# Seven products instead of eight in four pairs of chunks of the second feed-forward input product, on one Trainium2 core

## What is computed

```python
    h = rmsnorm_2(x, g_ffn[l])
    u = causal_dwconv(h @ w_up[l], ffn_conv_w[l]) + ffn_conv_b[l]   # w_up: 2048 x 11264, conv over 3 positions
    gate, val = jnp.split(u, 2, axis=-1)
    x = x + (jax.nn.silu(gate) * val) @ w_down[l]
```

## Time and profile before

| | before |
|---|---|
| median of three runs | 2409.65 us (2408.84 to 2410.35) |
| the profiled execution | 2408.56 us |
| its span, first to last instruction | 2406.8 us |
| TensorE busy in the span | 2396.3 us (10618 matmuls) |
| DVE busy | 1724.7 us (72%) |
| ACT busy | 1343.0 us (56%) |
| TensorE clock | 0.999 |

### The profile page before, as it was taken

How to read it: one execution, slowest core, us unless ns; L and a number is a source line. 1 busy time by engine, 2 the same in 40 slices (tenths; PEclk the granted TensorE clock), 3 DMA queues, 4 the chain that set the end, 5 groups by cost and what they waited for, 6 DMA issues and landing times.

```text
span 2406.8 us, 27970 instructions
## 1 busy us (share of the span) xinstructions
PE 2396.3 (100%) x10618; PEld 1984.3 (82%) x10618; DVE 1724.7 (72%) x2122; ACT 1343.0 (56%) x1641; POOL 190.1 (8%) x349
## 2 busy tenths in 40 slices
PE   9999999999999999999999999999999999999998
PEld 8888888888888888888888888888888888888887
DVE  7575555666778888669786865786577766678886
ACT  7555566445555555445455754555566666665554
POOL 0000000001000000000001110111111111110000
PEclk9999999999999999999999999999999999999999
DMA  8777666678767777776668777887788888886664
GB/s 276 224 222 231 195 189 185 215 240 247 221 215 220 230 222 218 226 220 210 198 223 274 247 236 218 254 246 236 236 244 248 243 242 239 243 239 208 219 217 158
DMA packets 155446, 545.86 MB, mean 227 GB/s; under 512 B 20144, under 2 KB 20656, under 8 KB 155184
## 3 DMA queue, kind: packets, MB, share of 16 engines
q1 hardware_dynamic: 131552, 470.91, 62.2%
q0 software_dynamic: 23184, 72.37, 11.4%
q10 hardware_dynamic: 576, 0.79, 0.1%
HBM read 505.72 MB, written 38.27 MB: 226 GB/s over the span
## 4 chain that ended last, share of the span: by engine, by line
PE 93%; DVE 4%; DMA 1%; ACT 1%; issue 1%; SPq 0%; ACTq 0%; DVEq 0%
PE ps L1851 92%; DMA raw<-in_w_ffn_in 1%; DVE wl L1287 1%; DVE tmp L1315 0%; DVE wl L1324 0%; ACT wh L933 0%; ACT wh L957 0%; ACT tmp L973 0%; DVE gated_lo L1301 0%; DVE tmp L1318 0%; DVE tmp L1320 0%; DVE ps L1393 0%; PE ps L1989 0%; DMA XG<-in_x 0%; DVE tmp L1592 0%
## 5 line engine op out<-in xcount | busy, mean ns | idle before, releaser
L1287 DVE TENSOR_TENSOR wl<-raw,wh 128x1024 fp32r<-128x1024 f32 x794 | 966.0, 1222 | 620.4 <-ACT wh L933 619.0
L933 ACT CAST wh<-raw 128x1024 fp32r<-128x1024 f32 x794 | 829.2, 1049 | 769.4 <-PE ps L1851 760.5
L1851 PE MATMUL ps<-wh,x4g_hi 128*128 128x512 f32 x704 | 273.9, 389 | 0.0
L1851 PE MATMUL ps<-wl,x4g_hi 128*128 128x512 f32 x704 | 273.9, 389 | 0.0
L1851 PE MATMUL ps<-wh,x4g_lo 128*128 128x512 f32 x704 | 273.9, 389 | 0.0
L1851 PE MATMUL ps<-wh,x1g_hi 128*128 128x512 f32 x592 | 230.3, 389 | 0.0
L1851 PE MATMUL ps<-wl,x1g_hi 128*128 128x512 f32 x592 | 230.3, 389 | 0.0
L1851 PE MATMUL ps<-wh,x1g_lo 128*128 128x512 f32 x592 | 230.3, 389 | 0.0
L1851 PE MATMUL ps<-wh,h_hi 128*128 128x512 f32 x576 | 225.2, 393 | 0.6 <-ACT wh L938 0.6
L1851 PE MATMUL ps<-wh,h_lo 128*128 128x512 f32 x576 | 223.8, 391 | 0.0
L1851 PE MATMUL ps<-wl,h_hi 128*128 128x512 f32 x576 | 223.4, 390 | 0.0
(11 more groups left out here) (378 smaller groups left out, 3954.6 us busy)
## 6 DMA issues: line engine op xcount, KB each, us to landing
raw<-in_w_in SPq DMA_DIRECT2D x196, 512.0 KB, 4.3
raw<-in_w_ffn_in SPq DMA_DIRECT2D x176, 512.0 KB, 4.3
raw<-in_w_up SPq DMA_DIRECT2D x176, 512.0 KB, 4.7
raw<-in_w_ffn_out SPq DMA_DIRECT2D x88, 512.0 KB, 4.2
raw<-in_w_down SPq DMA_DIRECT2D x88, 512.0 KB, 4.2
rows<-Y POOLq DMA_DIRECT2D x67, 512.0 KB, 4.9
Z<-rows POOLq DMA_DIRECT2D x268, 128.0 KB, 5.0
raw<-in_w_o SPq DMA_DIRECT2D x32, 512.0 KB, 4.3
```

The costliest lines, as they stand in the source:

```text
L933: e.copy(wh[:, i % RING, :], raw[:, slot, :]).then_inc(rounded, 1)
L1287: e.tensor_tensor(wl[:, r, :], raw[:, i % RAW, :], wh[:, r, :].bitcast(F32), ALU.subtract).then_inc(remainder, 1)
L1851: return e.matmul(dst, weights, x, start=start, stop=stop, skip_group_check=True)
```

## The change

Pairs 1, 3, 5 and 7 of the up product (chunks 2, 3, 6, 7, 10, 11, 14, 15) are laid out side by side, with units at row pairs 4 and 6 of the eight. In pair 1 the two units are steps 3 and 5 (counted from 0) of six common steps; in the others they are steps 1 and 3 of four. The four banks 4 to 7 take the pair, 0 to 3 the shared products. The up stage gets tiles of its own for bases, sums and x forms. `shared_bank` is planned in the step s of `plan_up`, before `UP_LATE` is added; `UP_LATE` moves what follows chunk 3 three steps later, chunks 6, 10 and 14 one, chunks 7, 11 and 15 two, leaves chunk 1 at four, and takes the two steps of chunk 2 away. The host reorders the weights of the four pairs. The down product's first pair now waits for `up_rows` 14 and 15 for its banks.

```diff
-SEVEN = {"gated": (4, 6), "out1": (8, 10, 12, 14, 16, 18), "down": (8, 10, 12, 14, 16, 18)}
+SEVEN = {"gated": (4, 6), "up": (4, 6), "out1": (8, 10, 12, 14, 16, 18), "down": (8, 10, 12, 14, 16, 18)}
...
+UP_PAIRS = (1, 3, 5, 7)
+UP_ORDERS = {1: (0, 1, 2, 4, 3, 6, 5, 7), 3: (0, 4, 1, 6, 2, 3, 5, 7), 5: (0, 4, 1, 6, 2, 3, 5, 7), 7: (0, 4, 1, 6, 2, 3, 5, 7)}
+UP_TAILS = {1: 6, 3: 4, 5: 4, 7: 4}
+UP_LATE = {1: 4, 2: 0, 3: 3, 6: 1, 7: 2, 10: 1, 11: 2, 14: 1, 15: 2}
...
+        up_hi = view("up_hi", [P, 3, 512], o_b + 28 * K, FR)
+        up_lo = view("up_lo", [P, 3, 512], o_b + 74 * K, FR)
+        up_sums = view("up_sums", [P, 4, 512], o_b + 80 * K)
+        up_xs_hi = view("up_xs_hi", [P, 2, 4, P], o_b + 34 * K, FR)
+        up_xs_lo = [view(f"up_xs_lo{i}", [P, 4, P], o_b + at * K, FR) for i, at in enumerate((38, 72))]
...
@@ -533,7 +545,9 @@
         def plan_up(n):
             def after(s, chunk):
                 chunk.drained = [("up_rows", n)]
-                s += (0, 4, 2)[n] if n < 3 else 0
+                s += UP_LATE.get(n, 0)
+                if n // 2 in UP_PAIRS:
+                    do("shared_bank", "up", n)
...
-        for n in range(2, 22):
-            last_up = product(t["w_up2"], "N", "ffn2", PAIRS16, ("up", n), plan_up(n), n)
+        plan_x_sums("up", len(granules), 0)
+        for q in range(1, 11):
+            if q in UP_PAIRS:
+                cleared = [[("pool_out", 1)], [("x_split", 1, 1)]] if q == 1 else [[("up_rows", 2 * q - 4 + n)] for n in range(2)]
+                product_side_by_side(t["w_up2"], "up", q, 4, UP_ORDERS[q], UP_TAILS[q], [plan_up(2 * q), plan_up(2 * q + 1)], 0, cleared,
+                                     ("shared_out", "shared_sums", "shared_last"))
+                continue
+            for n in (2 * q, 2 * q + 1):
+                last_up = product(t["w_up2"], "N", "ffn2", PAIRS16, ("up", n), plan_up(n), n)
+                if q - 1 in UP_PAIRS:
+                    last_up.cleared = [("shared_out", "up", q - 1)]
...
-            cleared = ([("pool_out", 1)], [("x_split", 1, 1)]) if q == 0 else ([("shared_out", "down", 0)],) * 2
+            cleared = ([("up_rows", 14)], [("up_rows", 15)]) if q == 0 else ([("shared_out", "down", 0)],) * 2
...
+        def up_at(n):
+
+            return at("shared_bank", "up", n) if n // 2 in UP_PAIRS else product_of("up", n)
...
-                    e.wait_ge(*product_of("up", n))
+                    e.wait_ge(*up_at(n))
...
+                    elif unit.pair.stage == "up":
+                        if unit.pair.q > UP_PAIRS[0]:
+                            e.wait_ge(*at("shared_bank", "up", 2 * unit.pair.q - 3))
...
+                    if stage == "up":
+                        e.tensor_tensor(up_xs_lo[0][:], up_out[:, 0], up_xs_hi[:, 0].bitcast(F32), ALU.subtract)
+                        e.tensor_tensor(up_xs_lo[1][:], up_out[:, 1], up_xs_hi[:, 1].bitcast(F32),
+                                        ALU.subtract).then_inc(done[name], 1)
+                        continue
...
-                    n, = args
-                    bank0, bank1 = banks(named["gated", n])
-                    e.wait_ge(*product_of("gated", n))
+                    stage, n = args
+                    tile_sums = tile_sums_of[stage]
+                    bank0, bank1 = banks(named[stage, n])
+                    e.wait_ge(*product_of(stage, n))
```

More of the change, by code:

```diff
@@ L810, in two_slots @@
             return x[:, i % RING:i % RING + 2, :].rearrange("p r c -> p (r c)")
-        bases = {"gated": (gated_hi, gated_lo), "out1": (base_hi, base_lo), "down": (base_hi, base_lo)}
-        x_places = {"gated": (gated_in, gated_out), "out1": (xs_in, xs_out), "down": (xs_in, xs_out)}
+        bases = {"gated": (gated_hi, gated_lo), "out1": (base_hi, base_lo), "up": (up_hi, up_lo),
+                 "down": (base_hi, base_lo)}
+        x_places = {"gated": (gated_in, gated_out), "out1": (xs_in, xs_out), "up": (up_in, up_out),
+                    "down": (xs_in, xs_out)}
         def all_three(x):
@@ L821, in x_forms @@
                 return [[x[:, unit.place, n] for x in (gated_xs_hi, gated_xs_lo)] for n in range(4)]
+            if unit.pair.stage == "up":
+                return [[x[:, n] for x in (up_xs_hi[:, unit.place], up_xs_lo[unit.place])] for n in range(4)]
             k = 2 * unit.p
@@ L956, in scalar @@
                     e.wait_ge(*at("sums", i))
+                    tile_sums = tile_sums_of[seven[i].pair.stage]
                     e.copy(two_slots(wh, i), tile_sums.rearrange("p k c -> p (k c)")).then_inc(done[name], 1)
@@ L972, in scalar @@
                     for k, place in enumerate((0, 3, 2, 1)):
-                        e.copy(tile_sums[:, place, :], ps[:, pair.shared + k, :]).then_inc(done[name], 1)
+                        e.copy(tile_sums_of[stage][:, place, :], ps[:, pair.shared + k, :]).then_inc(done[name], 1)
                 elif name == "first_hi":
@@ L1357, in vector @@
                     stage, q = args
-                    p1, p7, p6, _ = (tile_sums[:, k, :] for k in range(4))
+                    p1, p7, p6, _ = (tile_sums_of[stage][:, k, :] for k in range(4))
                     e.wait_ge(*at("shared_out", stage, q))
@@ L1364, in vector @@
                     stage, q = args
-                    _, second, first, p5 = (tile_sums[:, k, :] for k in range(4))
+                    _, second, first, p5 = (tile_sums_of[stage][:, k, :] for k in range(4))
                     e.wait_ge(*at("shared_sums", stage, q))
@@ L1390, in vector @@
                     else:
-                        b = named["gated", n].bank
-                        e.wait_ge(*at("shared_last", "gated", n // 2))
+                        b = named[stage, n].bank
+                        e.wait_ge(*at("shared_last", stage, n // 2))
                         e.tensor_tensor(ps[:, b:b + 2, :], ps[:, b:b + 2, :], tile_sums[:, 2:4, :], ALU.add).then_inc(done[name], 1)
```

35 lines of the change are left out of this document (21 added, 14 removed).

## The result

| | before | changed |
|---|---|---|
| median | 2409.52 us (4 runs) | 2439.19 us (4 runs, 2436.54 to 2440.95) |
| profiled execution | 2408.56 us | 2440.95 us |
| span | 2406.8 us | 2439.1 us |
| matmuls | 10618 | 10594 |
| TensorE clock | 0.999 | 0.994 |

The changed kernel is 1.0121 times as long (95% interval 1.0109 to 1.0133): **29.7 us slower**, where 2436, 26.5 more, was forecast.

The account below looks back on a forecast made before the run. TensorE was taken to bound the kernel, 93% of the chain that ended last. 31.9 us of waits less 5.4 saved gave +26.5 on 2409.65, thus 2436 us; range 2411 to 2450.

Parts of the forecast that it names:

- sum of waits: TensorE waits in all four pairs: 3.0 in pair 1, 12.7 in pair 3, 16.2 in pairs 5 and 7.
- Saving: Eight steps of the pairs, 21 matmuls each in place of 24: 5.4 us saved on TensorE's path.
- up_rows 9 at 12.2: Pair 5: up_rows 9 ends 12.2 us after TensorE starts the pair, wanted at 5.4: a wait of 6.8 us.
- the walk's first event: Pair 5: up_first 6 on ACT starts 23.0 us before TensorE begins the pair.
- this costs nothing: Weight fetches: SP's wait for base_lo, with later fetches behind it, delays no weight TensorE needs; cost 0.
- Second units of pairs 5 and 7: Second seven-product step of each pair: TensorE, already 6.8 late, waits 1.2 us more for base_lo or forms_lo.
- Pair 3: Waits of 0.1 us at the second granule, 6.9 at the first unit, 5.7 at the second: 12.7 us.
- Pair 1: No wait at its units; three late splits behind it of 0.6, 1.25 and 1.1 us: 3.0 us.
- B: Rival: the walked waits hold and the clock falls in the long waits: 2446 us; chance 0.20.
- A: Rival: the walked waits hold at the high clock: 2436 us, by itself 2424 to 2442; chance 0.52.
- the opening's 2.4 us: Kernel start: 12 matmuls read as low-clock lose 2.4 us, taken as price for each of four long waits, 9.6 in all.

Follow-up runs that it names:

- e9: Changed kernel plus 28 further matmuls on a zero tile ahead of the wait for up_rows in pairs 3, 5 and 7: 2439.13 us.
- e7: Changed kernel with up_rows put first in its step wherever its chunk isn't late: 2435.97 us.
- e2: Changed kernel with all four pairs laid out as pair 1, units at steps 3 and 5, second chunk's followers three steps late: 2455.44 us.
- e13: Changed kernel with most of the depthwise convolution left out (output wrong) and up_rows first in its step: 2425.96 us.
- e3: Changed kernel with only pair 5 side by side, its lateness kept, pairs 1, 3 and 7 plain: 2408.18 us.
- e8: Changed kernel with only pairs 3 and 7 side by side, lateness 0 and 1 steps, up_rows first in its step: 2409.94 us.
- e11: Changed kernel with only pairs 3 and 7 side by side, lateness 1 and 2 steps, up_rows in its old place: 2408.63 us.
- e4: Changed kernel with pairs 3, 5 and 7 side by side, pair 1 plain, lateness one step less: 2417.82 us.
- e1: Changed kernel with what follows chunks 6, 7, 10, 11, 14 and 15 planned one step earlier: 2432.85 us.
- e5: Changed kernel with only pair 1 side by side, pairs 3, 5 and 7 plain: 2420.05 us.
- e12: Changed kernel with only pairs 3 and 7 side by side, second unit at step 4 and five common steps: 2418.44 us.
- e10: Changed kernel with most of the depthwise convolution left out for every chunk (output wrong), order kept: 2429.31 us.

## Why the forecast was right

The mechanism was right: TensorE stops at the first base products of pairs 3, 5 and 7 for `up_rows`, which stands behind a lagging chain. That the number came so near (29.7 for 26.5) is in part luck. The sum of waits, 30.6 for 31.9, holds because terms that were too small (late splits, pair 5's first unit) meet terms that were too large (all the second units), and the low clock, 6.9 us, wasn't in it at all.

**Saving.** 24 matmuls fewer at 0.2267 us; the rest of the kernel takes the same time within 1.0 us. Right.

**"up_rows 9 at 12.2".** It ended at 13.5, in the order forecast: the wait of 8.1 for 6.8. Nearly all of the 1.3 us was there at the walk's first event: up_first 6 starts at t = -21.6, not -23.0. ACT's rows ahead of it:

```profile
1891.35 1.05 ACT L964 CAST wh<-raw 128x1024 fp32r<-128x1024 f32 x1 [3.28 <-DMA raw<-in_w_up]
1895.00 1.05 ACT L964 CAST wh<-raw 128x1024 fp32r<-128x1024 f32 x1 [2.61 <-DMA raw<-in_w_up]
1896.46 1.05 ACT L964 CAST wh<-raw 128x1024 fp32r<-128x1024 f32 x1 [0.41 <-DMA raw<-in_w_up]
...
1899.69 2.08 ACT L1258 ACTIVATE tmp<-FW,cst 128x256 f32<-128x256 f32 x4
```

The casts wait for weights, 3.3, 2.6 and less. In ACT's view of the product such waits sum to 15.7 us in 11 times; before there were none. What failed is "this costs nothing" on the fetches, which looked at one slot inside the walk only. e9, the kernel kept busy, is the counterpart: there the cast ahead of up_first 6 waits for TensorE and for no weight, and the walk comes out to 0.1 us. Its pair 5 begins at 1923.6:

```profile
1899.64 1.05 ACT L966 CAST wh<-raw 128x1024 fp32r<-128x1024 f32 x1 [0.63 <-PE ps L1901]
1900.60 2.08 ACT L1260 ACTIVATE tmp<-FW,cst 128x256 f32<-128x256 f32 x4
...
1935.23 0.68 ACT L1245 ACTIVATE tmp<-ps,small 128x512 f32<-128x512 f32 x1
```

up_first 6 at -23.05 and the end of `up_rows` 9 at 12.3, for -23.0 and 12.2. Why the weights were late is argued and not shown: the splits before had been late and then quick, so the fetches that they release came in a bunch, and the DMA engines were 98% busy from 1890 to 1900 (76% in the kernel before); but in e9 they were 96% busy in the same 10 us. Pair 7 shows no such shift at its first unit: 6.9 measured, 6.8 walked.

**Second units of pairs 5 and 7**, 1.2 us forecast, 0 measured. What failed isn't the walk of ACT and DVE but the pace it gave to TensorE: at the low clock TensorE came 2.3 and 2.6 us later. e9 kept the clock up, and the waits were there, 1.6 us each.

**Pair 3.** First unit right (6.9, 6.7). The 1.5 at its second granule for 0.1 and the 2.7 at the second unit for 5.7 are, as I read it, one size wrongly split: lag is paid once, wherever TensorE meets it first, and the low clock (2.0 us) covers a part. In all pair 3 waits 11.0 us for 12.7.

**Pair 1.** Late splits at the three places forecast, 4.5 for 3.0: the first was 2.0, not 0.6. The order is the forecast's (up_rows 2 waits 1.7 us for the adds onto its bank, L1436, and the cast of the late split ends behind it at 1781.2); which term of the walk was too short stays open.

**Clock.** B, which I gave 0.20, happened, and A's number held. The clock fell in each of the three long waits, for 10, 12 and 13 matmuls. The Trainium skill (TensorE: Matmul & The Clock Gate, "Part 1: The HAM clock gate") says that an idle TensorE is throttled; the trace agrees (granted 0.50 to 0.51 behind the waits of 6.7, 8.1 and 6.9 us). What was wrong in B was to add the price in full: the opening's 2.4 us for each is the right size (2.0, 2.3 and 2.6), but most of it isn't lost where TensorE would wait next anyway (e9). Forecast A plus that price three times would have been 2443; measured were 2439. One reading behind the price is weaker than it was told: the low level of the opening was read from matmuls 0.42 us apart. They are as far apart as those at granted 0.50 here, but the profile's own row for 5.5 to 10.5 us gives a granted clock of 1.00.

**The reading as a whole.** That TensorE stops for `up_rows` is shown by the trace and by e7. That its place is the cause is only half true: e2 took the bank's wait away and was slower, e7 and e13 moved much of it to the second unit. What goes with the cost in most of the runs is the distance between chains. A pair with no other near it and only one distance of five steps between chains about it costs about what it saves (e3, e8, e11: within 0.1% of before). With three chains five steps apart, or with pairs in a row, a pair makes the kernel 3 to 12 us longer, its saving counted in (e4 9.2 us in three pairs, e1 24.3 and e7 26.5 in four, e5 10.6 in one, e2 46.8 in four). e12 doesn't fit this rule: its chains stand as far apart as in e11, and it costs 8.5 us in two pairs. There it was the adds of the shared products that met a chain. So the distance is a first look, and the order of the rows decides.

**Where my expectations of the runs failed** (e1, e2, e4, e5, e7, e9, e10, e12, e13: nine of twelve), the kernel was always slower than expected. In most of them I took a wait as gone when its cause was, and it came back at the next place where ACT and DVE hand work to each other.

What stays open: why the stretch ahead of the product differs by up to 4.6 us between profiled executions, why the weights came late before pair 5, and whether a layout exists in which all four pairs gain.

## What to carry to other kernels

Average load says little for a chain: DVE at 75% of the product was in no trouble by its sum, while serial hand-overs of 15.5 us, in places only 13.6 us apart, went with 30 us of waits of TensorE. Before work is put on idle engines, list for each stretch what every engine has in order, from which event it can start and when it is needed, and look at the place where the chains stand closest. A wait taken away from one place counts only once the next place has been walked too.

## What the hardware showed that I had not expected

The waits from 3.6 to 8.1 us in the changed product were each followed by the low clock, for 6 to 14 matmuls (0.427 us each for 0.227). Among the shorter ones the length doesn't say whether it comes. Two waits of 3.3 us in e7 (1931.9 and 1945.3) and one of 2.5 us in e13 weren't followed by it, nor any of the waits of 2.1 us and less in the changed kernel. But one of 2.3 us in e2 (1925.8), with no wait of over 0.3 us for 40 us ahead of it, was: granted 0.52 from 1926.5 to 1929.8, 7 matmuls. So were 2.2 us in e10, 2.6 us in e7 and 2.3 us in e5, each behind another wait.

In a stretch where other engines were behind, the low clock cost next to nothing: 28 needless matmuls in each of three waits, which kept the clock up there, left the median where it was (2439.13 for 2439.19).
